# Seven delta outputs turned by VectorE in the next iteration, and a modulation tile moved into the levels

## What is computed

```python
mod = (cond @ mod_w[i] + mod_b[i])[:, None, :]       # 2048 x 12288, sliced in six
proj = h @ w_in                                      # q, k, v, z of 32 value heads
...
o = gated_delta_rule(q, k, v, g, beta)               # heads x chunks of tokens, with an inverse
o = o * lax.rsqrt(jnp.mean(o * o, -1, keepdims=True) + NORM_EPS)
o = (o.astype(h.dtype) * norm_w) * jax.nn.silu(z.reshape(B, S, GDN_V_HEADS, HEAD_DIM))
return o.reshape(B, S, GDN_DV) @ w_out
```

## Time and profile before

| | |
|---|---|
| median of 3 runs | 2680.88 us (2679.38 to 2681.06) |
| profiled execution | 2680.55 us, span 2678.9 us |
| TensorE busy | 2628.5 us, 98% of the span |
| VectorE busy | 1997.6 us, 75% |
| ScalarE busy | 1221.8 us, 46% |
| GpSimd busy | 865.7 us, 32% |
| DMA | mean 206 GB/s |

### The profile page before, as it was taken

One profiled execution on the slowest core, in us unless ns is written; L12 is line 12 of the kernel. 1 busy time (PEld: TensorE's weight loads), 2 busy tenths in 40 slices (PEclk: granted clock), 3 DMA queues, 4 the chain that ended last, 5 costly groups with the idle time before them and its releaser, 6 DMA issues.

```text
span 2678.9 us, 44567 instructions
## 1 busy us (share of the span) xinstructions
PE 2628.5 (98%) x16843; PEld 2205.9 (82%) x16843; DVE 1997.6 (75%) x2523; ACT 1221.8 (46%) x1604; POOL 865.7 (32%) x646
## 2 busy tenths in 40 slices
PE   6999999999999999999999999999999999999998
PEld 4798899899887888888888888899777778888887
DVE  1487887788798687777777777689999996655554
ACT  2365556545665445343343343354333334444344
POOL 1076777777767404500000000014555550000000
PEclk8999999999999999999999999999999999999999
DMA  9966776776676776666666666655555555666664
GB/s 364 361 222 216 232 244 217 233 236 220 211 250 202 229 202 221 190 193 189 189 192 191 188 190 193 189 160 174 169 170 168 173 176 180 191 189 187 190 204 153
DMA packets 283972, 552.47 MB, mean 206 GB/s; under 512 B 16881, under 2 KB 54322, under 8 KB 282674
## 3 DMA queue, kind: packets, MB, share of 16 engines
q1 hardware_dynamic: 263488, 473.49, 57.2%
q0 software_dynamic: 19472, 76.06, 8.0%
q10 hardware_dynamic: 866, 0.80, 0.1%
HBM read 548.19 MB, written 2.10 MB: 205 GB/s over the span
## 4 chain that ended last, share of the span: by engine, by line
PE 82%; DVE 14%; DMA 2%; issue 1%; SPq 1%; ACT 0%; DVEq 0%
PE pg L1201 40%; PE pd L1201 18%; PE pg L930 5%; PE pg L943 4%; PE pg L1188 4%; DVE pd L2068 3%; DVE arena L2068 2%; PE pg L962 2%; DVE arena L2142 1%; DMA wr<-in_gdn_w_in 1%; PE pd L856 1%; DVE arena L2302 1%; DVE arena L2234 1%; DVE arena L2237 1%; DVE arena L2208 1%
## 5 line engine op out<-in xcount | busy, mean ns | idle before, releaser
L1794 ACT ACTIVATE wh<-wr 128x1024 fp32r<-128x1024 f32 x616 | 652.9, 1061 | 927.0 <-PE pg L1201 581.4
L2341 DVE TENSOR_TENSOR wl<-wr,wh 128x1024 fp32r<-128x1024 f32 x615 | 771.5, 1266 | 381.4 <-ACT wh L1794 378.1
L670 POOL TENSOR_TENSOR wl<-wr,wh 128x1024 fp32r<-128x1024 f32 x195 | 485.3, 2497 | 266.3 <-ACT wh L1575 127.3
L1201 PE MATMUL pg<-wh,hh 128*128 128x512 f32 x1344 | 528.9, 394 | 0.3 <-DVE hl L2417 0.3
L1201 PE MATMUL pg<-wl,hh 128*128 128x512 f32 x1344 | 527.3, 392 | 0.0
L1201 PE MATMUL pg<-wh,hl 128*128 128x512 f32 x1344 | 525.7, 391 | 0.0
L1575 ACT ACTIVATE wh<-wr 128x1024 fp32r<-128x1024 f32 x216 | 227.8, 1057 | 324.9 <-PE pg L943 163.5
L1201 PEld LDWEIGHTS pg<-wh,hh 128*128 128x128 f32 x1344 | 252.5, 188 | 59.5 <-DVE wl L2341 2.4
L943 PE MATMUL pg<-hh,wh 128*128 128x256 f32 x1024 | 299.9, 293 | 0.8 <-ACT arena L1635 0.8
L1201 PEld LDWEIGHTS pg<-wh,hl 128*128 128x128 f32 x1344 | 252.4, 188 | 56.4
L1201 PEld LDWEIGHTS pg<-wl,hh 128*128 128x128 f32 x1344 | 252.3, 188 | 54.4
(11 more groups left out here) (451 smaller groups left out, 4873.1 us busy)
## 6 DMA issues: line engine op xcount, KB each, us to landing
wr<-in_w_in SPq DMA_DIRECT2D x224, 512.0 KB, 3.8
wr<-in_ffn_w_gu SPq DMA_DIRECT2D x176, 512.0 KB, 3.8
wr<-in_gdn_w_in SPq DMA_DIRECT2D x128, 512.0 KB, 4.4
arena<-in_mod_w POOLq DMA_DIRECT2D x60, 1024.0 KB, 6.6
wr<-in_ffn_w_down SPq DMA_DIRECT2D x88, 512.0 KB, 4.6
arena<-in_mod_w SPq DMA_DIRECT2D x32, 1024.0 KB, 13.6
wr<-in_gdn_w_in SPq DMA_DIRECT2D x128, 256.0 KB, 3.2
wr<-in_gdn_w_out SPq DMA_DIRECT2D x56, 512.0 KB, 4.7
```

The lines of the kernel that those rows point to most:

```text
L670: nc.gpsimd.tensor_tensor(wl[c % RING][:], wraw[c % 4], wh[c % RING][:].bitcast(F32), ALU.subtract)\
L1201: m = nc.tensor.matmul(halves(bank)[:, h, :], act[x][:, k0 + k, h * P:(h + 1) * P], w[s][:, k, :], skip_group_check=True, start=(first and ...
L1794: a(wh[c % 4][:], wraw[c % 4], ACT.Copy).then_inc(s_hc, 1)
L2341: v.tensor_tensor(wl[c % 4][:], wraw[c % 4], wh[c % 4][:].bitcast(F32), ALU.subtract).then_inc(s_lc, 1)
```

## The change

- TensorE's eight output transposes fall away in iterations 0 to 6; only the last iteration keeps them. *gram* no longer waits for the multiplication.
- VectorE turns `oz` itself in iterations 1 to 7 for the iteration before: 16 transposes of 32 x 256 into `Xb`, then the multiplication, now from SBUF. They stand at t = 0, behind L2199 and ahead of L2208. Iteration 0 is written out ahead of the loop.
- Modulation tile 0 (halves 0 and 1), which stood at that place, moves to t = 3, and halves 2 to 9 each one step later. The whole first column block accumulates in PSUM.
- `md0` and `o0` become two steps (t = 15 and 16), so that all later steps have a number one higher. Half 10 goes from t = 11 to 14, half 11 from t = 11 to 15, half 12 stands at 15, 13 at 16, 14 and 15 at 17. Turns of v move from t = 4 and 8 to later ones.
- A semaphore `s_og` counts the outputs; the readers of `oT` wait for it.
- In the last iteration two of the low parts of the outputs (`o_low`) are made later.
- GpSimd's order of work is not changed.

```diff
-MOD_HALVES = {0: (0, 1), **{t: (t - 1,) for t in range(3, 11)}, 11: (10, 11), 14: (12,), 15: (13,), 16: (14, 15)}
-V_TURNS = {3: (0, 2), 4: (2, 4), 8: (4, 6), 9: (6, 8), 10: (8, 10), 12: (10, 14), 13: (14, 16)}
-LATE_LOWS = (0, 1, 2, 4, 6)
+MOD_HALVES = {3: (0, 1), **{t: (t - 2,) for t in range(4, 12)}, 14: (10,), 15: (11, 12), 16: (13,), 17: (14, 15)}
+V_TURNS = {3: (0, 2), 9: (2, 4), 10: (4, 6), 11: (6, 8), 12: (8, 14), 13: (14, 16)}
+LATE_LOWS = (0, 1, 2, 5, 15)
...
-                if it:
-                    pe.wait_ge(s_v, bv)
...
-                V("on")
-                for c in range(TT):
-                    for h in range(VH):
-                        m = tr(pdv(1)[:, c, h], oz[:, c * VH + h, :])
-                m.then_inc(s_ot, 1)
+                if it == NIT - 1:
+                    V("on")
+                    for c in range(TT):
+                        for h in range(VH):
+                            m = tr(pdv(1)[:, c, h], oz[:, c * VH + h, :])
+                    m.then_inc(s_ot, 1)
...
                 PEw("md0")
                 mod_sum(it, 0)
+                yield
                 PEw("o0")
...
             def finish(it):
-                dve.wait_ge(s_ot, it + 1)
+                dve.wait_ge(s_v, it * len(VO) + VO["on"])
+                for n in range(16):
+                    i, q = slice(32 * (n // 4), 32 * (n // 4) + 32), slice(32 * (n % 4), 32 * (n % 4) + 32)
+                    m = v.transpose(Xb[q, :, i], oz[i, :, q])
+                link(m)
                 v.tensor_scalar(oT[:, bass.ds(it * VH, VH), :].rearrange("p h (c t) -> p c h t", c=TT),
-                                pd[1][:].rearrange("p (c h t) -> p c h t", c=TT, h=VH), vc[:, V_NW:V_NW + 1], None,
-                                ALU.mult).then_inc(s_v, 1)
+                                Xb.rearrange("p (c h) t -> p c h t", c=TT), vc[:, V_NW:V_NW + 1], None, ALU.mult)\
+                    .then_inc(s_og, 1)
...
-                    held = range(4, 16) if 2 <= half < 8 else range(8) if 8 <= half < 12 else range(0)
+                    held = range(16) if half < 8 else range(4) if half < 10 else range(0)
...
-                for t in range(18):
+                for t in range(19):
                     next(steps, None)
+                    if t == 0 and not first:
+                        finish(j - 1)
```

More of the change, by code:

```diff
@@ L54 @@
            *[f"{a}{s}" for s in LEVELS for a in (("x", "t", "us") if s < 32 else ("x", "t"))],
-           "x64", "u64", "md0", "o0", "rhs1", "o1", "oz", "md1", "on", "og")
+           "x64", "u64", "md0", "o0", "rhs1", "o1", "oz", "md1", "on")
 AO = order("rnq", "rn", "exp", "kg", "u1", "z", *[f"u{s}" for s in LEVELS], "v0", "s", "qs", "v1", "qkv", "rstd")
@@ L430, in build @@
         s_ot = sem("s_ot")
+        s_og = sem("s_og")
         s_zh = sem("s_zh")
@@ L736, in _ @@
             restart()
-            pool.wait_ge(s_v, NIT * len(VO))
+            pool.wait_ge(s_og, NIT)
             pool.dma_start(res, A["x"][0].rearrange("(t p) n -> p t n", p=P)).then_inc(s_res, 16)
@@ L1262, in _ @@
                 if t == 2:
-                    pe.wait_ge(s_v, NIT * len(VO))
+                    pe.wait_ge(s_og, NIT)
                     for i in range(2):
@@ L1808, in o_high @@
             def o_high(i):
+                act.wait_ge(s_og, i + 1)
                 k = slice(4 * i, 4 * i + 4)
@@ L1819, in _ @@
             high(0, 0, 2)
-            act.wait_ge(s_v, (NIT - 1) * len(VO) + VO["og"])
             o_high(7)
@@ L2285, in finish, with finish_last @@
             def finish(it):
-                dve.wait_ge(s_ot, it + 1)
-                v.tensor_scalar(oT[:, bass.ds(it * VH, VH), :].rearrange("p h (c t) -> p c h t", c=TT),
+                dve.wait_ge(s_v, it * len(VO) + VO["on"])
[3 more added lines that the diff above has]
+                link(m)
+                v.tensor_scalar(oT[:, bass.ds(it * VH, VH), :].rearrange("p h (c t) -> p c h t", c=TT),
+                                Xb.rearrange("p (c h) t -> p c h t", c=TT), vc[:, V_NW:V_NW + 1], None, ALU.mult)\
+                    .then_inc(s_og, 1)
+            def finish_last():
+                dve.wait_ge(s_ot, 1)
+                v.tensor_scalar(oT[:, (NIT - 1) * VH:, :].rearrange("p h (c t) -> p c h t", c=TT),
                                 pd[1][:].rearrange("p (c h t) -> p c h t", c=TT, h=VH), vc[:, V_NW:V_NW + 1], None,
-                                ALU.mult).then_inc(s_v, 1)
+                                ALU.mult).then_inc(s_og, 1)
             def o_low(i):
@@ L2309, in mods, with iteration @@
                 for half in MOD_HALVES.get(t, ()):
-                    held = range(4, 16) if 2 <= half < 8 else range(8) if 8 <= half < 12 else range(0)
+                    held = range(16) if half < 8 else range(4) if half < 10 else range(0)
                     mod_half(it * 8 + 32, half // 2, half % 2, held)
-            def iteration(j):
+            def iteration(j, first=False):
                 steps = delta(j, True)
-                for t in range(18):
+                for t in range(19):
                     next(steps, None)
+                    if t == 0 and not first:
+                        finish(j - 1)
                     if t == 5:
@@ L2327, in iteration @@
                     mods(j, t)
-                    if isinstance(j, int) and t == 16:
+                    if isinstance(j, int) and j == NIT - 2 and t == 17:
                         o_low(0)
                         o_low(1)
-            with dve.Fori(0, NIT - 2) as j:
+            iteration(0, True)
+            with dve.Fori(1, NIT - 2) as j:
                 iteration(j)
-                finish(j)
             iteration(NIT - 2)
-            finish(NIT - 2)
             def low(j, per, c):
@@ L2356, in _ @@
             steps = delta(NIT - 1, False)
-            for t in range(18):
+            for t in range(19):
                 next(steps, None)
+                if t == 0:
+                    finish(NIT - 2)
                 v_turns(t)
@@ L2366, in _ @@
                     mod_half(LATE, n // 2, n % 2, range(2, 12) if 1 <= n < 6 else range(0))
-                if t == 16:
+                if t == 17:
                     for i in range(3):
@@ L2371, in _ @@
             link(v.tensor_tensor(modt[:, 32:92], modt[:, 32:92], vc[:, V_MODB + 32:V_MODB + 92], ALU.add))
-            finish(NIT - 1)
+            finish_last()
             low(0, 0, 2)
```

## The result

The changed kernel takes 2793.65 us (median of 4 runs, 2791.61 to 2794.3) against 2680.63 for the kernel before in the same session: a ratio of 1.0421, 95% interval 1.0403 to 1.0439. Slower, as forecast, but by 113 us where the forecast said 88.6, and so 1.65 us past the upper end of the range.

The account below looks back on a forecast made before the run. TensorE is busy nearly all the time, with no slack in VectorE's chain from *rows* to the first level step. Six iterations of 12.2 (73.2), with 9.8 and 5.6, make 88.6; 2680.55 + 88.6 = 2769 us, range 2742 to 2792.

Parts of the forecast that it names:

- The stall at chunk 19: TensorE waits 7.7 us for GpSimd's `low`, queued behind the load of tile 7, which waits for VectorE's late tile 5.
- some 11: Sign in the profile after: GpSimd waits some 11 us for VectorE before its load of tile 7.
- The first level step: Starts 1.9 us later: VectorE's output of 8.2 at t = 0, less tile 0's 5.9 and 0.4 for a dropped multiplication.
- The multiplication: VectorE's SBUF to SBUF multiplication of the output at t = 0, taken as 1.0 us, ends 0.75 and twice 1.32.
- the tile's 5.9 us: Time tile 0 filled on VectorE at t = 0, taken off because the output takes its place.
- The waits at chunks 9 and 13: TensorE stalls 0.6 and 0.9 us for `low` behind loads of tiles 2 and 4: 1.5 together, ends 0 and 3.
- What the clock costs behind the wait at the first level step: Some 2.5 us idle there; its clock cost was taken as absorbed by stalls at chunks 9 and 13, adding nothing.
- The clock behind chunk 19: Half clock when TensorE resumes after the 7.7 us stall costs 1.7 us, ends 0 and 3.4.
- Iteration 7: Last iteration: 7.8 us more at the first level step and chunks before it, less a 2.2 wait: 5.6.
- clock low twice as long: Rival: half clock behind the chunk 19 stall lasts twice as long, 7 x 1.7 more, 2781 us; chance 0.14.
- The 2.5 us: The skill's figure for eight blocks transposed on VectorE; the forecast cited it but used 7.1 us for the 16 turns.

Follow-up runs that it names:

- out_only: The kernel before with only the outputs transposed and weighted by VectorE at t = 0, all tiles and turns of v unmoved: 2730.83 us, ratio 1.0186.
- tiles_only: The kernel before with only the new places of modulation tiles and turns of v, the output staying on TensorE: 2763.97 us, ratio 1.0313.
- fill_lvl: The changed kernel with 3 unused fp32 matmuls on TensorE ahead of the first level step in iterations 1 to 7: 2788.16 us, ratio 1.0402.
- fill8_c19: The changed kernel with 8 unused fp32 matmuls on TensorE behind the v0 step, before chunk 19, in iterations 0 to 6: 2785.45 us, ratio 1.0391.
- best1: The changed kernel with 4 turns early, `low` of chunk 6 held behind the multiplication, half 11 earlier, GpSimd's loads of tiles 2 to 7 later: 2704.05 us, ratio 1.0087.
- best2: best1 with modulation halves 12 and 13 moved behind the four VectorE operations (L2268) that a TensorE step waits for: 2709.0 us, ratio 1.0105.

## Why the prediction was right and where it was wrong

- **The stall at chunk 19** was right in place, cause and size: 7.8 us for 7.7, in the mean of seven (7.64 to 7.68 and once 8.48), GpSimd 10.9 us at the load, once 11.7, for "some 11".
- **The first level step** came 2.3 us later, forecast 1.9. The size was right by two errors that cancel. The multiplication took 2.6 us in place of 1.0, since it meets a `low` in all seven iterations. In its stead the two operations of L2214 no longer meet one (2.54 us before, as L2215 they take 1.39). That the tile's 5.9 us were themselves half standing still, *out_only* shows.
- **The waits at chunks 9 and 13** were mis-sized: forecast 1.5 together, and 2.5 where the clock is up (*tiles_only*, *fill_lvl*).
- **The step that failed** is the sentence "What the clock costs behind the wait at the first level step (some 2.5 us idle) is taken up by the stalls at chunks 9 and 13". The wait was 2.9 us. Half clock behind it made the next chunk 2.5 to 2.6 us longer in four of six iterations and 1.5 in one; in iteration 4 the clock stayed up. Of this the waits at chunks 9 and 13 took up 1.0 to 1.2 us and no more: the stretch to v0 took 49.0 to 49.2 us in those four, 48.1 in the fifth and 47.6 in iteration 4. So the stretch took 2.8 us more than before where the forecast had 0.9. These 1.9 us are half of what is missing per iteration (16.2 in the table against 12.2): 1.0 is the clock's net price, which the sum had at nothing (48.60 against 47.62 in *fill_lvl*), 0.9 the waits. The clock at this one wait is thus a quarter of the miss; the other quarters are the waits at chunks 9 and 13, the clock behind chunk 19, and the small terms below.
- **The clock behind chunk 19** was 1.7 in the sum and cost 2.2 (*fill8_c19*), 1.9 to 2.7 (2.5 in the mean) by the rows of iterations 1 to 5. With a stall 0.1 longer the stretch v0 to L1122 is 10.3 longer, forecast 9.4: 0.9 more.
- **The rest**: first level step 0.4, the two stretches behind L1122 0.7, with waits of *ssq* for VectorE's sum that I had not looked for (3.3 us in all).
- **Iteration 7**: forecast 5.6, measured 4.0. The first level step came 6.6 us later for a forecast of 7.8 (the wait, 5.4 us, is at a chunk ahead of it, for a low part of the output), the levels are 2.3 us shorter for 2.2, and the stretch behind the v0 step is 0.4 shorter.
- The rival "clock low twice as long" (2781) was nearest. It was wrong in the place: the second loss is at another wait. The 2.5 us that the Trainium skill's page "VectorE: DVE Perf Modes" (section "The three transpose paths") gives by its figure for eight blocks did not apply: 16 turns took 7.18 us.

Whether the output on VectorE can be made a gain is not settled. With the stalls repaired TensorE is the faster up to L1122, and VectorE's added work shows in the last third of the iteration, wherever I put it (*best1*, *best2*). How much of that would go without GpSimd's `low` beside it was not tried, and there is no time for a kernel that has the multiplication behind the transpose that the first level step waits for.

## What to carry to other kernels

Ask of each duration that goes into a sum what the neighbour on the shared ports did in that row: take the minimum, the median and the maximum of the form, and look up whether the moved operation will start behind or ahead of the other engine's. When a producer moves later, follow its buffer through the other engine's queue to whatever stands behind the load; and when such a queue is released, expect a row of catch-up operations, which can hold up others for longer than the stall itself. Price every idle stretch of TensorE that is as long as one behind which the profile already shows half clock, and count what is given back at the next wait.

## What the runs showed of the hardware

- VectorE operations with two inputs in SBUF, and a multiplication from SBUF to SBUF, stand still beside a GpSimd operation that started ahead of them, and GpSimd's next one can start first again: 0.75 us became 2.6 to 2.8 behind one `low`, and 7.5 to 9.8 with three or four of them in a row. Transposes of 32 x 256 were not touched: 16 took 7.18 us beside `low` too, none of 112 over 442 ns, and L2069 with an input in PSUM at most 757 ns.
- The same wait did not always bring the same clock. Behind a wait of 2.93 to 3.01 us the next chunk took 6.2 to 6.3 us in four iterations and 5.2 in iteration 5 (granted clock 0.66 from 718.65 to 723.50). In iteration 4 the wait was 2.94 us again, and the clock stayed at 2.4 GHz (1.00 from 612.12 to 615.82); the chunk behind it took 3.70 us:

```profile
612.12 0.69 PE L1070 MATMUL pd<-arena 64*64 64x64 f32 x32 [2.94 <-DVE arena L2227]
615.82 0.69 PE L1083 MATMUL pd<-arena 64*64 64x64 f32 x32
```
